# Expert stage: the low-part subtractions of VectorE done two chunks at a time

## The chip, the cores and the metric

One core of one Trainium2 chip runs the whole program. The time is device microseconds of one launch. The kernel before was timed three times: 1662.11 us in the median, 1661.32 and 1665.05 at the ends.

## The reference

One step of a transformer-like backbone over 512 latent tokens and 128 context tokens of width 1024: two kinds of attention, a gated merge, and then a mixture of 16 experts, of which each token uses two. The change touches only the experts:

```python
    for e in range(N_EXPERTS):
        gg, uu = jnp.split(t @ w_gate_up[e], 2, axis=-1)
        out = out + combine[:, e:e + 1] * ((jax.nn.silu(gg) * uu) @ w_down[e])
```

Everything is float32. `w_gate_up[e]` is 1024 x 1024 (4 MB), `w_down[e]` is 512 x 1024 (2 MB).

## The kernel before

The 1280 (token, expert) pairs are sorted by expert into tiles of 128 rows; in this run there are 20 tiles. A tile is worked on against three weight blocks of its expert: gate, up and down, 2 MB each. A block is four chunks (`NC_CH = 4`) of 128 x 1024 float32, 512 KB each. Blocks are numbered by `q`; `par = q % 2` names the buffers.

A float32 product is made of three fast passes: each operand is split into a rounded high part and the rest. For weights, a chunk goes through four steps, each with its own engine and queue:

1. SP loads it (`block_in`, line 660) into `w_raw` (even blocks) or `raw_odd` (odd blocks; the trace calls it w_raw_odd). Before it loads chunk c of block q it waits until the subtraction of chunk c of block q - 2 is done (line 659), as that frees the buffer. There are eight such buffers.
2. ScalarE casts it to `w_hi` (`split_hi_moe`, line 878), after the load has landed and TensorE has given back the slot of `w_hi` (semaphore `moe_used`). There are two blocks of slots.
3. VectorE subtracts, `w_lo = w_raw - w_hi` (`split_lo_moe`, line 1332), and adds to `lo_done`.
4. TensorE multiplies (`gate_up`, lines 1632 to 1634, and `down`, lines 1647 to 1649). Before each chunk it waits for that chunk's `lo_done`.

Every engine has its order written out by hand. In one tile VectorE does (`dve_tile`): the subtractions of the down block, `silu` (line 1344), the subtractions of the next tile's gate block, `times_up` (line 1349), `rest_x` (line 1337, the low part of the next tile's tokens), the subtractions of the next tile's up block, `rest_hidden` (line 1353). TensorE does (`pe_tile`): gate and up, `turn_x` (line 1618, transposes the next tile's tokens), the down product of the tile before, `turn_hidden` (line 1655). ScalarE does: the casts of down, `gate_tanh` (line 887), the casts of gate, `round_x` (line 882), the casts of up, `take_out` (line 892), `round_hidden` (line 896). TensorE starts a tile's gate product only after `rest_x` of that tile.

GpSimd first scatters the token rows to their tiles in memory (line 1833), then loads one tile of rows (line 1848) and stores one tile of results (line 1853) in each step, 512 KB each. The weight reloads that SP issues share the DMA engines with these. The subtractions of blocks 0 and 1 run ahead of the first tile.

The split of the earlier stages is another function (line 941), and isn't changed.

Of the kernel before, what the change touches and what calls it, by code (L numbers as in the profile page):

```python
# [20 lines left out]
F32 = mybir.dt.float32  # L21
# [4 lines left out]
ALU = mybir.AluOpType  # L26
# [26 lines left out]
NC_CH = 4  # L53
# [42 lines left out]
def hybrid_step(nc, t):  # L96

    with ExitStack() as ctx:
        def sb(name, shape, dt=F32, stack=ctx):
            return stack.enter_context(nc.sbuf_tensor(name, shape, dt))  # L100

        def sem(name):
            return ctx.enter_context(nc.semaphore(name))
# [30 lines left out]
        w_raw = sb("w_raw", [P, NC_CH, 2, CW])  # L134
        w_hi = sb("w_hi", [P, 2, NC_CH, 2, CW], F32R)
        w_lo = sb("w_lo", [P, 2, NC_CH, 2, CW], F32R)
# [3 lines left out]
        hi_done = sem("w_hi_done")  # L140
        lo_done = sem("w_lo_done")
# [22 lines left out]
        NB = len(blocks)  # L164
# [271 lines left out]
        raw_odd = sb("w_raw_odd", [P, NC_CH, 2, CW], F32, s4)  # L436
# [83 lines left out]
        def landing(q, half, c):  # L520

            if q % 2:
                return raw_odd[:, c], raw2_in[c], 16 * (half + 1)
            return w_raw[:, c], raw_in[c], 16 * (NB + half + 1)
# [410 lines left out]
        def _(dve):  # L935
# [391 lines left out]

            def split_lo_moe(block):
                q, par, _ = block
                for c in range(NC_CH):  # L1330
                    dve.wait_ge(hi_done, NC_CH * (NB + q) + c + 1)
                    dve.tensor_tensor(w_lo[:, (NB + par) % 2, c], landing(par, 0, c)[0], w_hi[:, (NB + par) % 2, c].bitcast(F32),  # L1332
                                      ALU.subtract).then_inc(lo_done, 1)

            def rest_x(tile, s):
                dve.wait_ge(xh_done, tile + 1 + OFF)
# [20 lines left out]
            def dve_tile(i, s, final):  # L1357
                tile, (gate, up, down) = 2 * i + 1 + s, step_blocks(i, s)
                split_lo_moe(down)
                silu(tile)  # L1360
                nq = 6 * i + 3 * s + 5
                if final:
                    split_lo_moe((nq, 1, 0))
                    times_up(tile, up[0])
                else:
                    split_lo_moe((nq, (3 * s + 5) % 2, 0))
                    times_up(tile, up[0])
                    rest_x(tile + 1, s)
                    split_lo_moe((nq + 1, (3 * s + 6) % 2, 0))
                rest_hidden(tile)  # L1370
# [573 lines left out]
```

## Time and profile before

| | us |
|---|---|
| median of the timed runs | 1662.11 |
| span of the profiled execution | 1662.6 |
| busy in it: TensorE matmul | 1336.0 |
| VectorE | 1085.6 |
| ScalarE | 705.8 |
| VectorE line 1332, from w_raw | 143.2 |
| VectorE line 1332, from w_raw_odd | 143.1 |
| all DMA, mean | 200 GB/s |

The profile is of one execution. An engine's busy time is what its instructions took, not what they cost the kernel: most of it lies beside other work. The expert stage runs from about 1164 to 1577 us of the span; stages before and after it have other limits. A row of the waits names an engine and line, whom it waited for, the sum in us, how often, and the longest. "Releaser" is who ended an idle time.

### The profile page before, as it was taken

The numbers are of one execution on the slowest core, as the hardware profiler recorded it, in microseconds if no ns is written. First come the engines' busy times: TensorE is split into PE (matmuls) and PEld (weight loads), VectorE is DVE, ScalarE is ACT, GpSimd is POOL, SyncE is SP. The second block draws the span as 40 slices with busy tenths as digits, with TensorE's granted clock in tenths as the row PEclk, the third lists the DMA queues.
The fourth block names the chain that finished last, engine by engine and source line by source line (L and its number), as shares of the span: only waits on it lengthen the run. The fifth ranks groups of instructions, "written<-read, shape, count | busy, mean of one in ns | idle before, by whom it ended". The sixth has DMA issues, their size and how long they took to land.

```text
span 1662.6 us, 21046 instructions
## 1 busy us (share of the span) xinstructions
PE 1336.0 (80%) x6852; PEld 1087.6 (65%) x6852; DVE 1085.6 (65%) x1891; ACT 705.8 (42%) x1008; POOL 250.3 (15%) x278
## 2 busy tenths in 40 slices
PE   2599999967999877889995999783299999999800
PEld 0377776655788766788884788563178887777600
DVE  6556552489822377755556634766289999999665
ACT  3523333232322366545444212002078787778600
POOL 0002111011120000000000331453300000000044
PEclk7799999989999999999997999985599999999955
DMA  6545555433473576611203884421889999999642
GB/s 229 167 139 191 193 181 182 147 116 100 146 236 110 151 176 154 180 41 59 73 17 104 298 297 134 166 89 63 316 291 393 392 392 393 392 392 392 258 177 88
DMA packets 152376, 333.05 MB, mean 200 GB/s; under 512 B 17595, under 2 KB 23259, under 8 KB 152299
## 3 DMA queue, kind: packets, MB, share of 16 engines
q1 hardware_dynamic: 123914, 233.22, 41.3%
q0 software_dynamic: 26944, 93.59, 16.1%
q10 hardware_dynamic: 1440, 5.24, 1.0%
q8 instruction: 45, 0.74, 0.2%
q14 instruction: 33, 0.26, 0.1%
HBM read 263.41 MB, written 68.58 MB: 200 GB/s over the span
## 4 chain that ended last, share of the span: by engine, by line
PE 50%; DVE 20%; DMA 13%; issue 9%; ACT 6%; POOL 1%; SPq 0%; ACTq 0%; POOLq 0%; DVEq 0%
PE psum_pair L1425 7%; PE psum_pair L1427 7%; PE psum_pair L1426 7%; DMA w_raw_odd<-in_w_gate_up 4%; DMA w_raw<-in_w_gate_up 4%; PE psum_pair L1518 4%; PE psum_pair L1505 3%; PE psum_pair L1557 3%; PE psum_pair L1558 3%; PE psum_pair L1559 3%; PE psum_pair L1495 3%; DVE w_lo L941 3%; DVE w_lo L1332 2%; ACT p_turned L375 2%; DVE minus_max L1101 2%
## 5 line engine op out<-in xcount | busy, mean ns | idle before, releaser
L941 DVE TENSOR_TENSOR w_lo<-w_raw,w_hi 128x1024 fp32r<-128x1024 f32 x124 | 146.5, 1222 | 152.0 <-ACT w_hi L715 150.2
L1425 PE MATMUL psum_pair<-w_hi,h_hi 128*128 128x512 f32 x520 | 212.3, 408 | 34.7 <-DVE w_lo L941 31.2
L1426 PE MATMUL psum_pair<-w_lo,h_hi 128*128 128x512 f32 x520 | 208.1, 400 | 0.0
L1427 PE MATMUL psum_pair<-w_hi,h_lo 128*128 128x512 f32 x520 | 208.1, 400 | 0.0
L1101 DVE TENSOR_REDUCE minus_max<-psum_pair 128x1 f32<-128x640 f32 (+1 forms) x160 | 114.3, 715 | 96.6 <-PE psum_pair L1495 96.0
L715 ACT CAST w_hi<-w_raw 128x1024 fp32r<-128x1024 f32 x124 | 124.2, 1048 | 120.8 <-DMA w_raw<-in_w_ada 61.5
L799 ACT ACTIVATE p_unnormed<-psum_pair,minus_max 128x640 f32<-128x640 f32 (+1 forms) x160 | 113.4, 709 | 142.2 <-DVE minus_max L1101 142.2
L1332 DVE TENSOR_TENSOR w_lo<-w_raw,w_hi 128x1024 fp32r<-128x1024 f32 x120 | 143.2, 1222 | 22.8 <-ACT w_hi L878 18.6
L1332 DVE TENSOR_TENSOR w_lo<-w_raw_odd,w_hi 128x1024 fp32r<-128x1024 f32 x120 | 143.1, 1221 | 12.0 <-ACT w_hi L878 8.4
L878 ACT CAST w_hi<-w_raw 128x1024 fp32r<-128x1024 f32 x120 | 123.4, 1051 | 45.4 <-DMA w_raw<-in_w_gate_up 26.2
L1425 PEld LDWEIGHTS psum_pair<-w_hi,h_hi 128*128 128x128 f32 x520 | 101.2, 195 | 63.4 <-issue 39.3
L878 ACT CAST w_hi<-w_raw_odd 128x1024 fp32r<-128x1024 f32 x120 | 123.7, 1050 | 35.2 <-DMA w_raw_odd<-in_w_gate_up 25.3
L1632 PE MATMUL psum_pair<-w_hi,expert_in_hi 128*128 128x512 f32 x320 | 129.9, 406 | 7.3 <-DVE expert_in_lo L1337 7.2
L1495 PE MATMUL psum_pair<-k_bundle,q_bundle 128*128 128x512 f32 (+1 forms) x576 | 126.3, 337 | 6.8 <-ACT p_unnormed L799 6.1
L1518 PE MATMUL psum_pair<-v_bundle,p_turned 128*128 128x64 f32 (+1 forms) x1008 | 131.4, 275 | 0.0
L1634 PE MATMUL psum_pair<-w_hi,expert_in_lo 128*128 128x512 f32 x320 | 128.0, 400 | 0.0
L1633 PE MATMUL psum_pair<-w_lo,expert_in_hi 128*128 128x512 f32 x320 | 128.0, 400 | 0.0
L1518 PEld LDWEIGHTS psum_pair<-v_bundle,p_turned 128*128 128x128 f32 x1008 | 122.9, 193 | 1.3
L1427 PEld LDWEIGHTS psum_pair<-w_hi,h_lo 128*128 128x128 f32 x520 | 100.9, 194 | 22.1
L1426 PEld LDWEIGHTS psum_pair<-w_lo,h_hi 128*128 128x128 f32 x520 | 101.4, 195 | 20.4
L1495 PEld LDWEIGHTS psum_pair<-k_bundle,q_bundle 128*128 128x128 f32 x576 | 87.2, 191 | 14.6 <-issue 7.9
L726 ACT ACTIVATE turned_staging<-psum_pair 128x1024 f32<-128x1024 f32 (+1 forms) x38 | 36.3, 957 | 105.2 <-PE psum_pair L1453 105.2
(267 smaller groups left out, 2424.7 us busy)
## 6 DMA issues: line engine op xcount, KB each, us to landing
w_raw<-in_w_gate_up SPq DMA_DIRECT2D x80, 512.0 KB, 8.9
w_raw_odd<-in_w_gate_up SPq DMA_DIRECT2D x80, 512.0 KB, 9.4
w_raw<-in_w_in SPq DMA_DIRECT2D x52, 512.0 KB, 5.2
w_raw<-in_w_ada SPq DMA_DIRECT2D x48, 512.0 KB, 5.4
w_raw<-in_w_down SPq DMA_DIRECT2D x40, 512.0 KB, 9.5
w_raw_odd<-in_w_down SPq DMA_DIRECT2D x40, 512.0 KB, 9.5
expert_rows<-zeros POOLq DMA_DIRECT2D x27, 512.0 KB, 6.0
k_bundle<-k_transposed SPq DMA_DIRECT2D x28, 384.0 KB, 8.7
```

Source lines behind the costliest of these rows:

```text
L878: act.copy(w_hi[:, (NB + par) % 2, c], src).then_inc(hi_done, 1)
L941: dve.tensor_tensor(w_lo[:, b % 2, c], w_raw[:, c], w_hi[:, b % 2, c].bitcast(F32), ALU.subtract).then_inc(lo_done, 1)
L1101: dve.tensor_reduce(nmax[:, m % RR:m % RR + 1], spair(m)[:, 0:width(j)], AX.X, ALU.max, negate=True).then_inc(nb_done, 1)
L1332: dve.tensor_tensor(w_lo[:, (NB + par) % 2, c], landing(par, 0, c)[0], w_hi[:, (NB + par) % 2, c].bitcast(F32), ALU.subtract).then_inc(lo_ ...
L1425: pe.matmul(bank(n), a_hi, hi, start=first, stop=False)
L1426: pe.matmul(bank(n), a_hi, lo, start=False, stop=False)
L1427: last = pe.matmul(bank(n), a_lo, hi, start=False, stop=end)
L1495: last = pe.matmul(spair(m)[:, c0:c0 + w], q, k[:, g, k0:k0 + w], start=g == 0, stop=g == 1)
L1518: last = pe.matmul(obank(j)[:, 0:w], ptb[:, j % 2, k], vb[bi % 2][:, vt, 0:w], start=k == 0, stop=k == len(tiles) - 1)
L1632: pe.matmul(out, xt_hi[:, s, kk], hi, start=kk == 0, stop=False)
L1633: pe.matmul(out, xt_hi[:, s, kk], lo, start=False, stop=False)
L1634: last = pe.matmul(out, xt_lo[:, s, kk], hi, start=False, stop=kk == KD - 1)
```

## The change

In `split_lo_moe` the loop over four chunks becomes a loop over two pairs. One subtraction covers two neighbouring chunks, 2048 columns in each partition. It waits for the second chunk's cast, and adds 2 to `lo_done` at its end. SP's and TensorE's waits on `lo_done` are as they were.

```diff
             def split_lo_moe(block):
                 q, par, _ = block
-                for c in range(NC_CH):
-                    dve.wait_ge(hi_done, NC_CH * (NB + q) + c + 1)
-                    dve.tensor_tensor(w_lo[:, (NB + par) % 2, c], landing(par, 0, c)[0], w_hi[:, (NB + par) % 2, c].bitcast(F32),
-                                      ALU.subtract).then_inc(lo_done, 1)
+                buf = (NB + par) % 2
+                for c in range(0, NC_CH, 2):
+                    raw = (raw_odd if par else w_raw)[:, c:c + 2]
+                    dve.wait_ge(hi_done, NC_CH * (NB + q) + c + 2)
+                    dve.tensor_tensor(w_lo[:, buf, c:c + 2], raw, w_hi[:, buf, c:c + 2].bitcast(F32), ALU.subtract).then_inc(lo_done, 2)
```

## Rows read from the trace of the kernel before

**Rows 1.** Stretches: us, busy (x) of PE PEld DVE ACT POOL, PEclk, DMA share, GB/s

```profile
1166.00:1168.00 2.00, 0.00 (x0) 0.00 (x0) 2.00 (x2) 0.00 (x0) 1.69 (x2) 0.50 0.99 298
1218.00:1222.00 4.00, 4.00 (x12) 3.11 (x12) 1.39 (x2) 1.04 (x1) 0.00 (x0) 0.57 0.98 377
1222.00:1230.00 8.00, 8.00 (x36) 6.51 (x35) 6.46 (x6) 6.54 (x7) 0.00 (x0) 1.00 0.66 197
1236.00:1244.00 8.00, 8.00 (x38) 6.50 (x38) 7.35 (x7) 7.04 (x9) 0.54 (x1) 1.00 0.94 304
1244.00:1248.00 4.00, 4.00 (x19) 3.25 (x18) 3.96 (x4) 3.35 (x5) 0.28 (x1) 1.00 1.03 404
1300.00:1540.00 240.00, 236.36 (x1089) 191.42 (x1089) 219.81 (x206) 189.87 (x205) 13.85 (x26) 1.00 1.05 392
```

**Rows 2.** Waits, 1244 to 1290 us: who waited for whom, us, times, longest

```profile
ACT w_hi L878 <- PE psum_pair L1634: 4.7, 14, 0.4
ACT w_hi L878 <- DMA w_raw_odd<-in_w_gate_up: 0.4, 1, 0.4
```

**Rows 3.** Waits, 1300 to 1540 us

```profile
ACT w_hi L878 <- DMA w_raw<-in_w_gate_up: 24.2, 30, 1.6
ACT w_hi L878 <- DMA w_raw_odd<-in_w_gate_up: 23.3, 33, 1.5
...
ACT w_hi L878 <- PE psum_pair L1649: 0.3, 1, 0.3
```

**Rows 4.** The chain, early in the stage: start, us, what (turn_x of two neighbouring tiles)

```profile
1266.59 0.87 PE psum_pair L1618 x8
...
1284.69 0.87 PE psum_pair L1618 x8
```

**Rows 5.** Timeline of VectorE: start, us, line, what (down block, two tiles apart)

```profile
1388.54 4.63 DVE L1332 TENSOR_TENSOR w_lo<-w_raw_odd,w_hi 128x1024 fp32r<-128x1024 f32 x4 [0.25 <-ACT w_hi L878]
...
1426.00 4.63 DVE L1332 TENSOR_TENSOR w_lo<-w_raw_odd,w_hi 128x1024 fp32r<-128x1024 f32 x4 [0.24 <-ACT w_hi L878]
```

**Rows 6.** Groups by line (busy us, mean ns); tile expert_hidden (min/median/max ns)

```profile
L1332 DVE TENSOR_TENSOR w_lo<-w_raw,w_hi 128x1024 fp32r<-128x1024 f32 x120 | 143.2, 1222 | 22.8 <-ACT w_hi L878 18.6 <-issue 1.2
...
L1349 DVE TENSOR_TENSOR expert_hidden<-expert_hidden,psum_pair x19: 680/680/683, 1215.4 to 1549.2; 128x512 f32<-128x512 f32 x19
```

**Rows 7.** Timeline of ScalarE, tile 1: two neighbouring casts

```profile
1227.70 1.05 ACT L878 CAST w_hi<-w_raw_odd 128x1024 fp32r<-128x1024 f32 x1 [0.31 <-PE psum_pair L1634]
1229.10 1.05 ACT L878 CAST w_hi<-w_raw_odd 128x1024 fp32r<-128x1024 f32 x1 [0.35 <-PE psum_pair L1634]
```

**Rows 8.** Start of the stage: SP's timeline, and the chain's wait for the scatters

```profile
1166.06 3.82 SPq L660 DMA_DIRECT2D w_raw<-in_w_gate_up  x4
...
1178.94 11.37 DMA expert_rows<-rows,slot_of_pair
```

**Rows 9.** Timelines of ScalarE, VectorE and TensorE before tile 1's gate product

```profile
1213.19 1.05 ACT L878 CAST w_hi<-w_raw_odd 128x1024 fp32r<-128x1024 f32 x1 [0.35 <-PE psum_pair L1634]
...
1214.28 1.23 DVE L1332 TENSOR_TENSOR w_lo<-w_raw_odd,w_hi 128x1024 fp32r<-128x1024 f32 x1 [0.17 <-ACT w_hi L878]
1215.42 0.68 DVE L1349 TENSOR_TENSOR expert_hidden<-expert_hidden,psum_pair 128x512 f32<-128x512 f32 x1
...
1217.49 0.49 PE L1632 MATMUL psum_pair<-w_hi,expert_in_hi 128*128 128x512 f32 x1 [0.68 <-DVE expert_in_lo L1337]
```

**Rows 10.** DMA issues of 1236 to 1240, 1240 to 1246 and 1532 to 1557 us: KB, median us to landing

```profile
w_raw<-in_w_gate_up SPq DMA_DIRECT2D x4, 512.0 KB, 6.3
...
w_raw_odd<-in_w_gate_up SPq DMA_DIRECT2D x4, 512.0 KB, 6.9
...
w_raw<-in_w_down SPq DMA_DIRECT2D x4, 512.0 KB, 9.6
```

**Rows 11.** The chain at the end of the stage: start, us, what

```profile
1565.64 1.06 ACT w_hi L878
...
1567.87 0.69 DVE expert_hidden L1349
```

## The prediction

> **What bounds the kernel now.** I read the table of stretches first, then the waits of the expert stage in two parts, then the chain. Each token tile of that stage (20 tiles, 60 weight blocks, 240 chunks of 512 KB) needs three blocks of four chunks, and every chunk goes DMA, ScalarE cast (hi), VectorE subtraction (lo), TensorE. The table of stretches shows two different regimes [rows 1]. From 1300 to 1540 us the DMA engines are full (share 1.05, 392 GB/s); from 1222 to 1244 they are not (0.66 and 0.94, 197 and 304 GB/s), and from 1244 they are (404 GB/s). The waits agree: from 1244 to 1290 ScalarE's casts wait for TensorE to give back a w_hi slot (4.7 us on line 1634), from 1300 on they wait for DMA (24.2 and 23.3 us) and almost never for TensorE [rows 2, 3]. The period tells the same. TensorE's own tile takes 1284.69 - 1266.59 = 18.10 us [rows 4]; two tiles of VectorE take 1426.00 - 1388.54 = 37.46, or 18.73 us a tile [rows 5]. That is the DMA price: twelve weight chunks, one row tile loaded and one stored are 14 x 0.524 = 7.34 MB, and 7.34 MB / 392 GB/s = 18.73 us. So TensorE sets the pace until its tiles, at 7.34 MB / 18.10 us = 406 GB/s, have used up the lead of the loads; then DMA sets it to the end of the stage. VectorE is busy 219.81 of 240 us there [rows 1], nearly full but not last.
>
> **Part 1, the instructions.** 240 subtractions of 128x1024 become 120 of 128x2048. None of 2048 columns stands in the trace. From 512 columns (680 ns) to 1024 (1222 ns) is 542 ns [rows 6], so 1024 more cost 1084: 1222 + 1084 = 2.30 us; twice 1222, 2.44 us, is the upper bound. Four in a row take 4.63 us [rows 5], so they start (4.63 - 1.22) / 3 = 1.137 us apart: 0.085 us of each is under the next. A pair occupied 2 x 1.137 = 2.27 us and will occupy 2.30 - 0.085 = 2.22. The saving is some 0.06 us a pair, 7 us of VectorE in all and 0.4 us in a tile.
>
> VectorE's trace shows these starts 1.137 us apart although one lasts 1.222 us [rows 5, 6]. The Trainium skill, "VectorE: DVE Perf Modes", section "The TRN2 errata", says that SBUF latency is paid between instructions, once for each, and gives (N+151)/0.96 ns for an fp32 tensor_tensor. It agrees with the 1222 ns, and gives 2291 ns for 2048; section "The DRAIN you can't avoid" has the next operation wait for the pipe to empty. By these two a pair would save 151 cycles, 0.157 us, and all 120 would save 19 us; the row of four in a chain leaves only 0.06.
>
> As DMA is last in the long regime, none of this saving is on the path: I cost it at nothing. Its cover is the full DMA queue.
>
> **Part 2, the wait.** The merged subtraction waits for the second cast, and both chunks' lo_done come at its end. Behind it on VectorE queue silu, times_up, rest_x and rest_hidden; for lo_done wait TensorE (the block's matmuls) and SP, which reloads the raw buffers in that order. So the second chunk of a pair is released 2.30 - 1.22 = 1.08 us later where VectorE waits for casts, and the first by that plus the spacing of the casts. Where casts wait for TensorE they start 1229.10 - 1227.70 = 1.40 us apart [rows 7]: the first is late by 2.48, the pair on average by 1.78 us. Where VectorE works through a backlog the second is not late and the first by 1.1, on average 0.6 us.
>
> (a) Start of the stage. The four pairs of the two preloaded blocks delay SP's first reload, now at 1166.06 us, by 1.08 us, while the row scatters run whose last one holds back everything until 1190.3 [rows 8]. DMA is at 298 GB/s there [rows 1], some 94 below its later rate, so up to 1.08 x 298 / 392 = 0.8 us of transfer is pushed behind, or the scatters gain by the freer queue, as much. I take +0.2 (bounds -0.8 and +0.8).
>
> (b) Tile 1. The last cast of the gate block starts at 1213.19, lo follows at 1214.28, times_up at 1215.42, rest_x, and TensorE at 1217.49 [rows 9]. Nothing covers this: down has no work for TensorE yet. The pair starts at the same 1214.28 and ends 1.08 later: TensorE's first gate comes 1.08 us late, and all casts that wait for TensorE with it. Bounds 1.08 and 1.22, by the two prices of the instruction.
>
> (c) The DMA stream. Until about 1244 us its engines have spare capacity [rows 1], and capacity not used there is lost, since from there to the end they are full. The reloads that are paced by TensorE's slots then come 1.08 (from b) + 1.78 us later. So the full stream starts later and ends later; 1.78 is the term of this part. Bounds: 0.6 if VectorE mostly works through a backlog, 2.48 if the late first chunks decide; 0 is a rival below.
>
> (d) In the full regime the lag only takes transfers out of the queue. A reload takes 9.6 us from issue to landing late in the stage, and 12 / 18.73 x 9.6 = 6.2 of the 8 buffers are in flight. With an average lag of 0.6 to 1.8, say 1.6, they have 8.0 us and 5.1 are in flight. Issues of 1240 to 1246 us landed after 6.9 us [rows 10], and DMA moved 404 GB/s right behind them [rows 1]. I therefore cost it at nothing.
>
> (e) TensorE's steady path. rest_x of the next tile comes 1.1 us later behind the gate block's landing. It shifts TensorE once against DMA, and DMA stays last. Casts waited for TensorE there once, for 0.3 us [rows 3], so their slots are free in time by a margin that no row shows; were it under 1.1 us, the casts would be late by the rest once, not in each tile, and with 5 transfers in flight DMA would not run dry of it. I take nothing.
>
> (f) The tail. The last chunk lands, is cast at 1565.64, its lo is done in time for times_up at 1567.87, and turn, round_hidden and down follow [rows 11]. No transfer is left to hide it: + 1.08 us.
>
> **Sum.** 0.2 + 1.08 + 1.78 + 1.08 = 4.14 us. The profiled execution spans 1662.6 us; the median of the timed runs is 1662.11, which is 0.5 less, so the term carries over: 1662.11 + 4.1 = **1666.2 us**, 0.25% slower. About 0.2%, 3.3 us, is what a measurement of this kernel can tell from no change.
>
> **The rivals.**
> *The lag of the stream is hidden.* DMA share is 0.94 from 1236 to 1244 us [rows 1]. If the engines were really full there, the lag (c) and TensorE's (b) cost no transfer time: what is left is 0.2 + 1.08 = 1.3, or 1663.4 us. Against it stands the 304 GB/s, which is far from 392.
> *Troughs in the queue.* With 5.1 in flight on average (d), and two issued at a time, some 4 are left just before each refill. From 1236 to 1244 us, with latencies of about 6.3 us and 304 GB/s, 6.3 x 304 / 524 = 3.7 were in flight: at that depth DMA is not full. From 1244 us to the last landing there are 17 tiles of 18.73 us, with 51 blocks. If half of these had 1 us at 304 instead of 392 GB/s (0.22 us each), it adds 5.7 us: 1671.9; if all, 1677.6. It decides from some 4 in flight downward. For it speaks the arithmetic of (d), which is an average; against it the 404 GB/s at 6.9 us.
> *VectorE is the true pace (faster).* If the order of work on VectorE, busy 92% in the long regime [rows 1], and not DMA, set the releases that end last, the 0.06 us a pair would come back in each of the 17 tiles: 17 x 6 x 0.06 = 6.1 us, less the 0.2 + 1.08 + 1.08 of (a), (b) and (f): 1658.4 us. It decides once VectorE's own work, 219.81 / 240 x 18.73 = 17.2 us a tile, is longer than the DMA's 18.73, which it isn't; and a share of 1.05 speaks against it.
> By the skill's bubble the same rival would save 17 x 6 x 0.157 = 16 us.
>
> **How the numbers follow.** Forecast 0.50, hidden lag 0.29, troughs 0.16, faster 0.05. The forecast's own range, by the bounds of (a) to (c), is 1664.1 to 1667.9. The range of all runs from 1662.6, inside the hidden case, to 1672.0, the half-priced troughs. Slower by over 0.2% means above 1665.4: three quarters of the forecast (0.38) and the troughs (0.16), 0.54. Within 0.2%: the hidden case, a quarter of the forecast and a part of the faster one, 0.42. Faster: 0.04.
>
> **What would show it.** The merged group: 120 instructions of 2.30 us. TensorE's first gate of tile 1: its wait 1.1 us longer. The first stretch in which casts wait for DMA comes earlier than 1290 us, by several tiles. DMA from 1300 on: still 390 GB/s, with latencies near 8 us; the period still 18.73. The last landing 3 us later, and times_up of the last tile 4 us later. Wrong would be: a period above 18.8 (troughs), a last landing that hasn't moved (hidden lag), or a period below 18.7 (VectorE). The clock is a risk that I don't price: TensorE's granted clock is 0.57 in the mean from 1218 to 1222 us, so mostly at the lower level of 1.2 GHz [rows 1], right after its idle time before 1217 us, and that idle time gets 1.08 us longer.

## The result and the profile after

The changed kernel takes 1667.19 us in the median (1665.34 to 1670.35), the kernel before on the same chips 1664.88 (1661.32 to 1668.39, 20 runs each). The ratio is 1.0018, 95% interval 1.0011 to 1.0025: 1.8 to 4.2 us slower, 3.0 in the middle. Forecast were 4.1 us more than before, in a range up to 1672. The profiled execution spans 1665.6 us, against 1662.6.

The page of the changed kernel, its groups by line (busy us, mean ns, idle before):

```profile
L1334 DVE TENSOR_TENSOR w_lo<-w_raw,w_hi 128x2048 fp32r<-128x2048 f32 x60 | 136.9, 2291 | 34.0 <-ACT w_hi L878 32.7
L1334 DVE TENSOR_TENSOR w_lo<-w_raw_odd,w_hi 128x2048 fp32r<-128x2048 f32 x60 | 136.7, 2289 | 20.4 <-ACT w_hi L878 20.4
```

VectorE got 12.7 us of work less (273.6 against 286.3 busy), and its idle time ahead of these lines grew from 22.8 + 12.0 to 34.0 + 20.4 us: it waits for casts for all that it saved and 7 us more. The stretches of the changed kernel, with the columns of [rows 1]:

```profile
1222.00:1230.00 8.00, 8.00 (x36) 6.46 (x35) 5.87 (x4) 6.19 (x7) 0.00 (x0) 1.00 0.36 115
1236.00:1244.00 8.00, 8.00 (x38) 6.50 (x37) 7.39 (x5) 7.03 (x8) 0.54 (x1) 1.00 0.95 332
1300.00:1540.00 240.00, 235.05 (x1081) 190.14 (x1080) 211.72 (x129) 189.50 (x205) 13.91 (x26) 1.00 1.05 392
```

The long stretch is as full as in [rows 1], 392 GB/s. From 1222 to 1230 us DMA moved 115 GB/s, where it had moved 197: that is 0.66 MB less, of which 332 against 304 GB/s from 1236 to 1244 us gives 0.22 MB back. The issues of the long stretch (1300 to 1540 us; median us to landing) show what the lag took out of the queue:

```profile
w_raw<-in_w_gate_up SPq DMA_DIRECT2D x54, 512.0 KB, 7.0
w_raw_odd<-in_w_gate_up SPq DMA_DIRECT2D x48, 512.0 KB, 7.6
w_raw_odd<-in_w_down SPq DMA_DIRECT2D x28, 512.0 KB, 7.3
w_raw<-in_w_down SPq DMA_DIRECT2D x24, 512.0 KB, 7.2
```

In [rows 10] the late ones took 9.6 us. At 7.3 us, 12 / 18.73 x 7.3 = 4.7 transfers are in flight instead of 6.2 (both are estimates), and the rate is the same.

Tile 1 in VectorE's timeline, for [rows 9]:

```profile
1213.65 2.29 DVE L1334 TENSOR_TENSOR w_lo<-w_raw_odd,w_hi 128x2048 fp32r<-128x2048 f32 x1 [0.50 <-ACT w_hi L878]
1215.86 0.68 DVE L1350 TENSOR_TENSOR expert_hidden<-expert_hidden,psum_pair 128x512 f32<-128x512 f32 x1
1216.46 1.22 DVE L1338 TENSOR_TENSOR expert_in_lo<-psum_pair,expert_in_hi 128x1024 fp32r<-128x1024 f32 x1
```

The first wait of a cast for DMA comes in ScalarE's timeline at 1264.72 us, before it was at 1289.85:

```profile
1264.72 2.23 ACT L878 CAST w_hi<-w_raw_odd 128x1024 fp32r<-128x1024 f32 x2 [0.82 <-DMA w_raw_odd<-in_w_gate_up]
```

And the end of the stage, VectorE's timeline, for [rows 11]:

```profile
1568.67 2.29 DVE L1334 TENSOR_TENSOR w_lo<-w_raw_odd,w_hi 128x2048 fp32r<-128x2048 f32 x1 [0.27 <-ACT w_hi L878]
1570.88 0.68 DVE L1350 TENSOR_TENSOR expert_hidden<-expert_hidden,psum_pair 128x512 f32<-128x512 f32 x1
```

The stages ahead of the experts differ from one execution to the next by some us (VectorE's first expert subtraction starts at 1164.65 us before and at 1164.00 after, and between 1158 and 1165 in the runs below). So I measure everything from that subtraction on. The milestones, in us from its start, out of the timelines of VectorE and ScalarE:

| kernel | rest_x of tile 0 | rest_x of tile 1 | last cast | last times_up | last rest_hidden | last take_out | ratio to before |
|---|---|---|---|---|---|---|---|
| before | 33.06 | 51.37 | 400.99 | 403.22 | 405.28 | 412.06 | |
| changed | 33.09 | 52.46 | 403.52 | 406.88 | 408.94 | 415.72 | 1.0018 |
| peeled control | 33.78 | 51.65 | 401.20 | 403.42 | 405.48 | 412.26 | 0.9995 |
| pairs in the head | 33.23 | 52.59 | 401.40 | 403.62 | 405.68 | 412.46 | 1.0003 |
| pairs in tiles 1 to 4 | 33.71 | 51.66 | 402.83 | 405.06 | 407.12 | 415.46 | 1.0016 |
| pairs from tile 5 | 33.74 | 51.72 | 401.10 | 403.32 | 406.61 | 414.96 | 1.0000 |
| pairs in the tail | 33.69 | 52.06 | 400.00 | 403.36 | 405.42 | 413.73 | 1.0016 |
| trios from tile 5 | 33.32 | 51.54 | 427.11 | 429.33 | 432.60 | 439.38 | 1.0147 |
| quads from tile 5 | 33.56 | 51.99 | 464.57 | 466.79 | 468.85 | 475.63 | 1.0432 |
| delay of 5 us in tile 1 | 33.89 | 56.83 | 407.62 | 409.85 | 411.91 | 420.02 | 1.0036 |
| pairs, times_up moved | 33.37 | 52.60 | 403.33 | 401.54 | 408.74 | 415.52 | 1.0010 |
| before, both moves | 33.12 | 49.37 | 399.42 | 395.90 | 402.60 | 409.38 | 0.9966 |
| before, head move | 33.72 | 50.92 | 399.19 | 401.42 | 403.55 | 410.35 | 0.9992 |
| before, tail move | 33.74 | 51.75 | 402.98 | 398.56 | 405.78 | 412.59 | 0.9988 |

What follows the last take_out takes 85.8 to 86.4 us in all of them. One profile has its own chance in it: the eight kernels whose work up to tile 1's rest_x is that of before (before, control, pairs in tiles 1 to 4, pairs from 5, trios, quads, pairs in the tail, tail move) need 17.9 to 18.4 us from tile 0's rest_x to it, 18.1 in the mean, and two kernels with the same work up to the last tile, pairs in the tail and before with the tail move, have their last cast at 400.00 and 402.98 us. A shift of one us at the last cast is read from one profile alone with doubt.

Part of this chance is TensorE's clock at the start of tile 1's product. The same stretch in the kernel before, in the run with pairs in the tail and in the run with the head move (the third number from the right is the granted clock):

```profile
1215.00:1222.00 7.00, 5.16 (x17) 4.00 (x18) 4.15 (x5) 1.79 (x3) 0.20 (x1) 0.76 0.93 343
...
1215.00:1222.00 7.00, 5.76 (x26) 4.60 (x27) 4.48 (x5) 3.31 (x4) 0.00 (x0) 1.00 0.82 304
...
1215.00:1222.00 7.00, 7.00 (x32) 5.68 (x31) 5.19 (x6) 4.70 (x6) 0.00 (x0) 1.00 0.92 345
```

In ten of the fourteen profiles the granted clock is at the lower of its two levels (1.2 and 2.4 GHz) for 3.1 to 3.4 us of this product, in the run with the delay for 5.6 us, and in three (pairs in the tail, quads, head move) it stays at 1.00. What TensorE did just ahead of the product doesn't tell them apart: in the 3.9 us up to it, it was busy for 1.13 us in the kernel before and for 1.14 with pairs in the tail. By estimate, 3.4 us at half the clock cost 1.7 us.

The bytes show the same, and more steadily than the last cast. Summed over stretches of 5 us from the first subtraction, DMA had moved this much after 100 us:

| kernels | MB |
|---|---|
| single until there, lower clock (before, control, pairs from tile 5, trios, tail move) | 31.9 to 32.2, mean 32.06 |
| the same work, clock at 1.00 (pairs in the tail, quads) | 32.6, 32.6 |
| pairs in the head | 31.78 |
| pairs in tiles 1 to 4 | 31.51 |
| changed; pairs with times_up moved | 31.28; 31.27 |
| delay | 29.6 |
| both moves; head move | 33.04; 33.07 |

From 100 to 390 us every kernel with singles or pairs moved the same 113.7 MB. At 392 GB/s, 0.28, 0.55 and 0.78 MB less than 32.06 are 0.7 us for pairs in the head, 1.4 for pairs in tiles 1 to 4 and 2.0 for pairs everywhere.

### The profile page after: what moved, and what is told of

Read it like the earlier page. It is cut to its first block, busy times and chain, and to the rows that moved or that the text cites. A ratio compares the mean times of both kernels' runs of the same rounds, so it can differ in the third digit from the quotient of the medians.

```text
span 1665.6 us, 20934 instructions
## 1 busy us (share of the span) xinstructions
PE 1336.0 (80%) x6852; PEld 1087.5 (65%) x6852; DVE 1073.3 (64%) x1771; ACT 705.8 (42%) x1008; POOL 251.8 (15%) x278
## 4 chain that ended last, share of the span: by engine, by line
PE 49%; DVE 20%; DMA 15%; issue 8%; ACT 5%; POOL 1%; SPq 1%; ACTq 0%; DVEq 0%; POOLq 0%
DMA w_raw_odd<-in_w_gate_up 8%; PE psum_pair L1426 7%; PE psum_pair L1428 6%; PE psum_pair L1427 6%; DMA w_raw_odd<-in_w_down 4%; PE psum_pair L1519 4%; PE psum_pair L1506 3%; PE psum_pair L1558 3%; DVE w_lo L1334 3%; PE psum_pair L1559 3%; PE psum_pair L1560 3%; PE psum_pair L1496 3%; DVE w_lo L941 3%; ACT p_turned L375 2%; DVE minus_max L1101 2%
## 5 line engine op out<-in xcount | busy, mean ns | idle before, releaser
L941 DVE TENSOR_TENSOR w_lo<-w_raw,w_hi 128x1024 fp32r<-128x1024 f32 x124 | 146.6, 1222 | 151.5 <-ACT w_hi L715 150.1
L1334 DVE TENSOR_TENSOR w_lo<-w_raw,w_hi 128x2048 fp32r<-128x2048 f32 x60 | 136.9, 2291 | 34.0 <-ACT w_hi L878 32.7
L1334 DVE TENSOR_TENSOR w_lo<-w_raw_odd,w_hi 128x2048 fp32r<-128x2048 f32 x60 | 136.7, 2289 | 20.4 <-ACT w_hi L878 20.4
L878 ACT CAST w_hi<-w_raw 128x1024 fp32r<-128x1024 f32 x120 | 123.3, 1051 | 46.5 <-DMA w_raw<-in_w_gate_up 29.6
L1427 PEld LDWEIGHTS psum_pair<-w_lo,h_hi 128*128 128x128 f32 x520 | 101.3, 195 | 20.4
```

The source lines that it names most:

```text
L878: act.copy(w_hi[:, (NB + par) % 2, c], src).then_inc(hi_done, 1)
L941: dve.tensor_tensor(w_lo[:, b % 2, c], w_raw[:, c], w_hi[:, b % 2, c].bitcast(F32), ALU.subtract).then_inc(lo_done, 1)
L1334: dve.tensor_tensor(w_lo[:, buf, c:c + 2], raw, w_hi[:, buf, c:c + 2].bitcast(F32), ALU.subtract).then_inc(lo_done, 2)
L1427: pe.matmul(bank(n), a_hi, lo, start=False, stop=False)
```

## The experiments

All keep the kernel before but for what is named. The function takes the number of chunks in a subtraction:

```diff
+            def split_lo_moe(block, n, chunks=range(NC_CH)):
+                ...
+                for c in list(chunks)[::n]:
+                    raw = (raw_odd if par else w_raw)[:, c:c + n]
+                    dve.wait_ge(hi_done, NC_CH * (NB + q) + c + n)
+                    dve.tensor_tensor(w_lo[:, buf, c:c + n], raw, w_hi[:, buf, c:c + n].bitcast(F32), ALU.subtract).then_inc(lo_done, n)
```

and where a run has another n for some tiles, VectorE's loop is peeled:

```diff
+            for j in range(2):
+                for s in range(2):
+                    dve_tile(j, s, False, A)
-            with dve.Fori(0, last_pair) as i:
+            with dve.Fori(2, last_pair) as i:
                 for s in range(2):
-                    dve_tile(i, s, False)
-            dve_tile(last_pair, 0, True)
+                    dve_tile(i, s, False, S)
+            dve_tile(last_pair, 0, True, 1)
```

**The control** (A = S = 1).

> A control for the next three: VectorE's first two passes of the loop (tiles 1 to 4) are written out before it, and every subtraction is single, as in the kernel before. Every theory expects no difference: within 1 us of the kernel before, and the expert stage, from VectorE's first subtraction to the last tile's times_up (line 1349), 403.2 us as before.

Ratio 0.9995 (0.9986 to 1.0005), and 403.42 us to times_up. The peeled loop itself costs nothing.

**Pairs only in tiles 1 to 4** (A = 2, S = 1).

> Pairs only in tiles 1 to 4 (the two passes written out), single subtractions before and after. The main theory (lag lost where DMA isn't yet full): the expert stage becomes 1.4 to 1.8 us longer, the last weight landing moves by as much, and the tail behind it doesn't. The rival that the lag is hidden, because DMA was in effect full: 0. The rival that the loss is spread over the long stretch in which DMA is full: below 0.5 us, as only some 30 of its 240 us are touched.

Ratio 1.0016 (1.0008 to 1.0025). That is 1.3 to 4.2 us slower, though all tiles behind are those of before. The last cast comes at 402.83 us, 1.6 later than in the control; alone this would say little, as it is 402.98 with the tail move, but after 100 us DMA is 0.55 MB behind, 1.4 us, with the same clock. The hidden lag is refuted, and so is the spread loss: two passes of the loop hold the loss of the stream. (The last down product also ran 1.5 us longer in this profile, for which see the last section.)

**Pairs only from tile 5** (A = 1, S = 2).

> Pairs only in the loop from tile 5 on (up to the last tile's share, which is single), so in the stretch in which DMA is full. The main theory: 0 (within 0.4 us of the control), with a period of 18.73 us a tile and reloads that land after about 8 us, not 9.6. The rival of troughs or of a spread loss: 1.5 us or more. The rival that VectorE sets the pace: 5 us shorter.

Ratio 1.0000 (0.9990 to 1.0010); the last cast at 401.10 us, as in the control. The stretch and two of its issues:

```profile
1300.00:1540.00 240.00, 235.88 (x1086) 190.73 (x1084) 212.39 (x129) 191.23 (x207) 13.33 (x25) 1.00 1.05 392
...
w_raw<-in_w_gate_up SPq DMA_DIRECT2D x52, 512.0 KB, 7.3
w_raw_odd<-in_w_gate_up SPq DMA_DIRECT2D x50, 512.0 KB, 7.6
```

VectorE is 7.4 us less busy in these 240 than in [rows 1], the transfers land 2 us sooner, and the last cast and the bytes of the stretch are the same. Troughs and VectorE's pace are both refuted for pairs as far as DMA's stream goes. The end of the stage is another matter: the last gate product starts at 387.96 us instead of the control's 386.76, and the last rest_hidden is 5.51 us behind the last cast instead of 4.28, though the tail is single. TensorE runs 1.2 us later against DMA, and once DMA is done this shows. The ratio allows -1.7 to +1.7 us, so it neither confirms nor excludes this.

**Quads from tile 5** (A = 1, S = 4).

> As the run before it, but four chunks in one subtraction of 4096 columns (estimate 4.4 us). The average lag of a reload grows to some 4 us, and so 3.6 chunks would be in flight instead of 6.2. The main theory says that the full DMA queue covers 1.6 us of lag and not 4: the period rises by 0.4 to 1.5 us a tile, 5 to 20 us in all, and DMA falls below 380 GB/s. If the full stretch doesn't care for lag at all: below 1 us.

Ratio 1.0432 (1.0419 to 1.0446), 70 to 74 us, far over the 5 to 20 us. The profile is that of the fastest of the seven executions (1724.3 us; the median is 1733.6), with 63 us at the last cast. The direction was right, the size was not. The stretch, and the chain through one buffer's loop:

```profile
1300.00:1540.00 240.00, 205.27 (x867) 159.75 (x866) 168.91 (x74) 159.70 (x167) 10.67 (x20) 0.94 0.89 317
```

```profile
1399.12 7.86 DMA w_raw_odd<-in_w_down
1407.04 0.04 issue
1407.08 1.06 ACT w_hi L878
1408.18 0.04 issue
1408.23 4.44 DVE w_lo L1334
...
1414.69 6.84 DMA w_raw_odd<-in_w_gate_up
...
1421.62 1.06 ACT w_hi L878
...
1422.77 4.44 DVE w_lo L1334
...
1429.32 8.25 DMA w_raw_odd<-in_w_gate_up
```

From the last issue of a block to the last issue two blocks later it is 15.57 and 14.63 us: landing, cast, the whole subtraction, and then SP, which issues four loads one after the other, 0.63 us apart. Two blocks are two thirds of a tile, so a tile costs 1.5 x 15.1 = 22.7 us; VectorE's timeline has 23.1 us a tile in this profile. My estimate went by the mean lag and left out that the last load of a group is issued 1.9 us behind its release.

**Trios and a single from tile 5**, the size between:

```diff
-                for c in list(chunks)[::n]:
+                for c, n in ([(0, 3), (3, 1)] if n > 1 else [(c, 1) for c in chunks]):
```

> From tile 5 on each block is subtracted as three chunks at once (estimate 3.36 us) and then one; tiles 1 to 4, the head and the tail are single. Between the pairs, which cost nothing there, and the quads, which cost 61 us. The loop of one raw buffer may take two thirds of a tile, 12.49 us: here 7 us to land, 1.05 cast, the subtraction that it is in (up to 3.36) and its queue. The theory of that loop: just under 12.49, so 0 to 5 us slower. If the price grows in proportion to the lag (3.1 us on average, to some 5 in the quads): 30 us or more.

Ratio 1.0147 (1.0131 to 1.0162), 22 to 27 us, and 26 us at the last cast: neither estimate. The stretch and the chain:

```profile
1300.00:1540.00 240.00, 223.83 (x984) 178.70 (x983) 192.58 (x119) 177.24 (x187) 12.80 (x24) 0.96 1.00 358
```

```profile
1423.44 7.35 DMA w_raw<-in_w_gate_up
1430.89 1.05 ACT w_hi L878
1432.04 3.37 DVE w_lo L1334
1435.56 0.38 SPq L660
...
1437.07 7.93 DMA w_raw<-in_w_gate_up
```

The loop is 7.45 to the cast, 1.15 to the subtraction, 3.52 to SP, and 1.51 until the third load of the group is out: 13.63 us, or 20.4 a tile; VectorE's timeline has 20.57, and 7.34 MB / 20.57 us = 357 GB/s is what the stretch shows. So the loop accounts for the size once SP's serial issues are in it. For quads and trios this was worked out after the runs, from pieces of the chain itself; what it shows is that the chain goes round one buffer and which pieces the expectation had left out. For pairs the same sum, an estimate with the landing time of this row, is 7.45 + 1.15 + 2.4 + 0.6 = 11.6 us, under the 12.49 that DMA allows: by it some 0.9 us kept them free. No run lies between pairs and trios, so the place of the threshold isn't measured.

**Pairs only in blocks 0 to 3.**

> Pairs only in blocks 0 to 3, ahead of the loop. The main theory: the start of the stage isn't moved by it (a: 0), TensorE's first product of tile 1 is 1.07 us later, and this goes through to the end: the expert stage +1.1 to +1.3 us (the reloads behind blocks 2 and 3 lag too). The rival that a shift ahead of the full DMA stretch is hidden: 0.

rest_x of tile 1 is 19.36 us behind that of tile 0, against 18.31 before, as forecast; the last cast is only 0.4 us later, DMA is 0.28 MB behind after 100 us (0.7 us), and the ratio 1.0003 (0.9993 to 1.0014) allows -1.2 to +2.3 us. By itself this says little: the next run has the same shift, but five times as large.

**The delay in tile 1.**

```diff
             times_up(0, 1)
+            dve.wait_ge(xh_done, 2 + OFF)
+            for _ in range(4):
+                link(dve.tensor_tensor(xt_lo[:, 1].rearrange("p k q -> p (k q)"), pair[1][:],
+                                       xt_hi[:, 1].rearrange("p k q -> p (k q)").bitcast(F32), ALU.subtract))
             rest_x(1, 1)
```

> The kernel before, with VectorE's rest_x of tile 1 done five times instead of once (four dead repetitions of 128x1024, each waited for, some 1.25 us apiece), so TensorE's first product of tile 1 comes 5.0 us later and nothing else changes. The theory that time lost ahead of the full DMA stretch goes through to the end: last weight landing +4.5 to +5 us, kernel +5 us (ratio 1.003). The rival, that the loads' lead absorbs such a shift: below 2 us.

Ratio 1.0036 (1.0024 to 1.0048), 6.0 us slower; last cast at 407.62 us, 6.6 later than before and 4.6 later than the latest of the kernels with unchanged work. TensorE's timeline and the clock there:

```profile
1220.74 0.79 PE L1637 MATMUL psum_pair<-w_hi,expert_in_hi 128*128 128x512 f32 x1 [5.71 <-DVE expert_in_lo L1338]
```

```profile
1215.00:1220.00 5.00, 0.03 (x1) 0.00 (x0) 4.86 (x5) 0.60 (x1) 0.00 (x0) 0.63 0.95 351
1220.00:1225.00 5.00, 4.26 (x10) 3.40 (x11) 1.30 (x3) 1.04 (x1) 0.00 (x0) 0.50 0.03 10
```

The shift goes through in full, and the clock adds to it: TensorE starts the product at a granted 0.50 and spends 5.6 us of it at this level, where it spent 3.4 before; 2.2 us more at half the clock are 1.1 us, and with the 5.5 us by which rest_x came later that makes the 6.6. DMA is at 10 GB/s meanwhile: nothing can be loaded, as the casts, and behind them the buffers, wait for TensorE's slots, and this idleness is not made up for later.

**Pairs only in the tail.**

> Pairs only in the last tile's share behind the loop (the blocks of the last two down products). The main theory: the last weight landing doesn't move, times_up behind it comes 1.1 us later, and the whole kernel is 1.1 us longer. The rival that TensorE's own queue hides it at the end: 0.

From the last cast to times_up it takes 3.36 us, against 2.23 before: + 1.13. Ratio 1.0016 (1.0006 to 1.0026), so 1.0 to 4.3 us; the tail's own place is shown by the trace. In the profile the longer down product takes another 1.5 us, while the clock at tile 1, which stayed at 1.00, gave some 1.4 us back. The middles of the ratios of the three parts, head, tiles 1 to 4 and tail, add up to 5.8 us with pairs from tile 5 at nothing, the whole change to 3.0; each is uncertain by 1.4 to 1.7 us, so the ratios alone don't give the sizes of the parts.

**The changed kernel with times_up moved.**

```diff
                 if final:
-                    split_lo_moe((nq, 1, 0))
-                    times_up(tile, up[0])
+                    times_up(tile, up[0])
+                    split_lo_moe((nq, 1, 0), n)
```

> The changed kernel (pairs everywhere), with times_up of the last tile ahead of the last block's subtractions instead of behind them. The main theory: the 1.1 us of the tail goes away, as turn_hidden no longer waits for the last pair, and the down product needs its second half only later: 1.0 to 1.3 us faster than the changed kernel, so the expert stage is 2.4 us longer than before, not 3.6. If the tail isn't the place: no difference from the changed kernel.

Times_up comes 1.8 us ahead of the last cast, as meant, and yet the last rest_hidden is 5.41 us behind that cast, as in the changed kernel (5.42). Next late is the work in front: in ScalarE's timeline take_out waits for TensorE's down product of tile 18, and round_hidden stands behind it:

```profile
1561.54 1.05 ACT L878 CAST w_hi<-w_raw_odd 128x1024 fp32r<-128x1024 f32 x1 [0.27 <-DMA w_raw_odd<-in_w_down]
1565.40 1.01 ACT L892 COPY expert_out_rows<-psum_pair 128x1024 f32<-128x1024 f32 x1 [2.81 <-PE psum_pair L1651]
1566.31 0.60 ACT L896 ACTIVATE hidden_hi<-psum_pair 128x512 fp32r<-128x512 f32 x1
```

TensorE is late here by the 1.2 us that the run with pairs from tile 5 shows at its end. In the changed kernel both paths are late, that of times_up and that of TensorE, and to move one leaves the other. The expected 1.0 to 1.3 us didn't show in the trace (take_out at 415.52 against 415.72); the ratio, 1.0010 (1.0002 to 1.0019), overlaps that of the changed kernel.

**The kernel before with both moves**, times_up of the last tile as above, and in the head:

```diff
-            split_lo_moe((3, 1, 0))
+            split_lo_moe((3, 1, 0), 1, range(NC_CH - 1))
             times_up(0, 1)
             rest_x(1, 1)
+            split_lo_moe((3, 1, 0), 1, range(NC_CH - 1, NC_CH))
```

> The kernel before (single subtractions), with times_up and rest_x of tile 1 ahead of the last subtraction of block 3, and times_up of the last tile ahead of the last block's subtractions. By the main theory a gain of time ahead of the full DMA stretch goes through to the end as a loss does: TensorE's first product of tile 1 starts 0.8 to 1.1 us earlier, the tail gives 0 to 0.4 us: 0.8 to 1.5 us faster than the kernel before. By the rival that the stretch before 1244 us is hidden: at most 0.4 us.

Ratio 0.9966 (0.9953 to 0.9978): 5.6 us faster than before, more than expected, and the best kernel here. Its stage is only 2.7 us shorter (409.38 against 412.06). Of these, 2.0 are at tile 1's rest_x, and 1.2 of those are not from the move: ScalarE's last cast of block 3 is 47.38 us behind the first subtraction instead of 48.54, because TensorE came out of the lower clock sooner in tile 0: from 34 to 46 us behind the first subtraction it spent 3.6 us at the lower level, where it had spent 6.3. So two runs took the moves one by one.

> The kernel before, with only times_up and rest_x of tile 1 put ahead of the last subtraction of block 3. TensorE's first product of tile 1 comes 0.8 us earlier; if it goes through, the kernel is 0.8 us faster; if the 5.6 us of the run with both moves are real and from here, 3 us or more.

Ratio 0.9992 (0.9983 to 1.0001). rest_x of tile 1 is 17.20 us behind that of tile 0, 0.9 less than the 18.1 of the unchanged ones. After 100 us DMA is 1.0 MB ahead of 32.06, 2.6 us: the move explains 0.9, and the rest is of the size that the clock gives, as in this profile it stays at 1.00 at tile 1. The last cast at 399.19 us is therefore no measure of the move. Whether the move itself makes that likelier isn't shown.

> The kernel before, with only times_up of the last tile put ahead of the last block's subtractions. The last down product starts 1.1 us earlier behind the last landing: kernel 1.1 us faster. If the 5.6 us of the run with both moves are from here, 3 us or more.

Ratio 0.9988 (0.9977 to 0.9999). rest_hidden is 2.80 us behind the last cast instead of 4.29. The two together would give 3.3 us by their ratios; both in one kernel gave 3.7 to 7.8. That both together gain is measured; that it is more than the sum isn't, and the head move alone can't be told from no change.

## Why the prediction was right

**What bounds the stage**: right. Pairs where DMA is full cost the stream nothing, pairs where it isn't cost 1.4 us of transfers. One row was missing from the picture: between 1230 and 1236 us, a stretch that [rows 1] leaves out, DMA was full too (share 1.02, 367 GB/s), so the spare capacity lay in pieces on both sides of it.

**The instruction**: forecast 2.30 us, 2.29 measured. The start-to-start saving of 0.06 us a pair is there too: two pairs in a row take 4.50 us in VectorE's timeline, so they start 4.50 - 2.29 = 2.21 us apart, where the sum had 2.22 and two singles 2.27. That is 0.06 us a pair and not the 0.157 us of the other reckoning.

**(a) The start**: forecast +0.2, measured 0.0 in this pair (33.09 against 33.06 us to tile 0's rest_x). But the kernel before is the fastest here of the eleven profiles with single subtractions in blocks 0 and 1 (33.06 to 33.89, mean 33.58); the three with pairs have 33.09, 33.23 and 33.37. So the mean says 0.35 us earlier: within the bounds, and with the other sign. The text had named that case, the scatters gaining by the freer queue.

**(b) Tile 1**: forecast 1.08, measured 1.06 between the two rest_x in this pair, and 1.2 by the means (19.3 us in the three kernels with pairs there, 18.1 in the unchanged ones). The text called its block the gate block; block 3 is tile 1's up block, which stands ahead of rest_x in the head only. The sum isn't touched by the name. That the shift goes through is shown by the delay of 5 us, not by the 1 us alone.

**(c) The stream**: forecast 1.78. From tile 1's rest_x to the last cast it is 351.06, 351.17 and 350.73 us in the three kernels with pairs in the early tiles (changed, tiles 1 to 4, times_up moved), and 349.5 in the mean of nine with single ones there and no trios or quads (before, control, pairs from 5, pairs in the head, pairs in the tail, both moves, head move, tail move, delay), which scatter from 347.9 to 351.2. The difference is 1.5, with a standard error of 0.4 to 0.7. Against the six of the nine with the same 3.1 to 3.4 us at the lower clock it is 1.2, and the bytes say 1.4. So the term was perhaps a little large; it can't be told apart from 1.78.

**(d) The full queue**: forecast no cost, 8.0 us to landing and 5.1 in flight; measured none, 7.3 and 4.7. The margin was smaller than the text let expect: it argued from the number in flight, while in the trios the chain goes round the loop of one buffer, and at 3.4 us a subtraction that loop is the bound.

**(e) TensorE's steady path**: forecast nothing, and the period is the same (18.72 against 18.75 us in VectorE's timeline). But the shift isn't free at the end, where DMA no longer covers it: pairs from tile 5 alone put the last rest_hidden 1.2 us later behind the last cast (5.51 against 4.28 us). In the changed kernel this lies beside (f) and adds nothing to it, and it is what made the moved times_up useless: in the tail TensorE's own queue came last.

**(f) The tail**: forecast 1.08, measured 3.36 - 2.23 = 1.13. Two paths are late by about this much, that of times_up and that of (e); the forecast saw one.

**The clock**, named as a risk without a price: it cost nothing extra. TensorE spent 3.2 to 3.4 us at the lower level at tile 1, as before.

**The sum**: 0 + 1.1 + 1.4 + 1.1 = 3.7 us in this pair of profiles (415.72 - 412.06), where 4.1 were forecast. The spans differ by 3.0, as the earlier stages were 0.65 us shorter in the profile after. By the means over the profiles it is -0.35 + 1.2 + 1.2 to 1.5 + 1.13 = 3.2 to 3.5 us, and the timed ratio says 1.8 to 4.2. The mechanism is as it was told; (a) was sized too large by 0.2 to 0.55 us, and (c) by up to 0.6, which is within its error. That the absolute time was met so closely, 1667.19 against 1666.2, is luck: the median of three runs, 1662.11, lay 2.8 us below that of twenty, and the term of 4.1 us was 1.1 above the measured 3.0. From the median of twenty the forecast would have been 1669.0. The upper end of the forecast's own range comes to 1667.7 by the bounds of its terms (0.8 + 1.22 + 2.48 + 1.08), not to 1667.9.

**The chances**: slower by over 0.2% had 0.54 and within 0.2% had 0.42. The measured 0.18% lies within, so the likelier of the two classes didn't come, narrowly.

**The signs**: 2.29 us an instruction, 392 GB/s, the period, and times_up of the last tile 3.7 us later (403.22 to 406.88) came as told; the last cast moved by 2.5 us instead of 3. TensorE's first product of tile 1 starts 1.09 us later (53.93 against 52.84 us from the first subtraction), but its own wait reads 0.68 us in both profiles: the time went into the steps ahead of it. The first cast that waits for DMA came 25 us earlier, 1.3 tiles and not several.

What stays open: why the kernel with both moves is 3.7 to 7.8 us faster when its stage is 2.7 us shorter in the profile, and some of that is the clock.

## What to carry to other kernels

Merging instructions of an engine that isn't last buys nothing, and it delays by one cast and one instruction everything that waits for the first half: here the cost falls at the two ends of the stage and in the stretch in which the bounding resource isn't full yet, and none on the stream where it is. Before merging, add up the loop of one buffer: landing, each step on it, and the issues that one release sets free, one behind the other; if it stays under the buffer's share of the bound (here 11.6 of 12.49 us, by estimate), the merge is free in the steady part, and above it the price is paid in every cycle (20.6 and 23.1 us a tile instead of 18.7). And time lost at the start of a stage whose long part is bound by a full resource counts one for one, as the delay shows. Time won there should count too: both moves together gained 3.7 to 7.8 us where the merge lost 3.0, but how much of it is the moves and how much the clock isn't shown.

## What the runs showed of the hardware

The last down product, from rest_hidden to the copy behind it, takes 6.8 us in eight of twelve executions with singles or pairs, and 8.1 to 8.4 in the four others (pairs in tiles 1 to 4, pairs from tile 5, pairs in the tail, the delay). In the slower ones the granted clock fell in it, as in the kernel with pairs in the tail:

```profile
1568.00:1572.00 4.00, 2.50 (x8) 1.91 (x7) 0.69 (x1) 0.60 (x1) 0.35 (x1) 0.70 0.32 131
1572.00:1576.00 4.00, 4.00 (x17) 3.24 (x16) 0.00 (x0) 0.00 (x0) 0.00 (x0) 0.88 0.00 0
```

TensorE waits 1.5 to 2.05 us ahead of it in all of them, for hidden_lo, and in the kernel before the granted clock stayed at 1.00 from 1560 to 1580 us. What decides between the two isn't shown; it puts 1.5 us of chance into a single profile, half as much as the whole change.

At the start of tile 1's product the fall of the clock differs in the same way between executions with the same work up to there: 3.4 us at the lower level in the kernel before, the control, pairs from tile 5, trios and the tail move, and none with pairs in the tail and with quads. What decides isn't shown here either. In bytes moved after 100 us the difference is 0.55 MB, or 1.4 us.

Five loads in flight (an estimate from the landing time) moved as much as six: at 7.3 us to landing and at 9.6 the rate was 392 GB/s. With trios the rate fell to 358 GB/s and with quads to 317, while the medians to landing stayed at 6.3 to 7.5 and 6.0 to 6.9 us.
